# Three edits to the first layer of a fused three-layer kernel: gate projection placed before the recurrence, group norm regrouped, input squares summed by matmul

## The chip, the cores and the metric

The kernel runs on one core of a Trainium2 chip. The metric is device time in microseconds. Three executions took 2455.23, 2460.22 and 2460.65 us (median 2460.22). Five engines work side by side, each through its own queue in order, and meet through semaphores: TensorE (PE), VectorE (DVE), ScalarE (ACT), GpSimd (POOL) and SyncE (SP), which here only issues transfers.

## The reference

A sequence of 512 tokens of width 1024 goes through an RWKV-7 layer, an attention layer with forget gates and a hybrid layer, each with an MLP of width 4096. All is float32. Only the RWKV layer is changed. Cut to what matters:

```python
h = rmsnorm(x, g);  xx = shift(h) - h;  x_m = h + xx * mu[m]     # m: r w k v a g
r, k, v = x_r @ Wr, x_k @ Wk, x_v @ Wv
w = -softplus(-(w0 + tanh(x_w @ w1) @ w2)) - 0.5;  decay = exp(-exp(w))
a = sigmoid(a0 + (x_a @ a1) @ a2)
g = sigmoid(x_g @ g1) @ g2                    # rank 160, the output gate
kk = normalised(k * k_k);  k = k * (1 + (a - 1) * k_a);  b = kk * a
y  = scan(S -> S*w - (S@kk) b + v k, read with r)
y  = (y - mean) * rsqrt(var + eps) * lnx_w + lnx_b              # per head of 64
y  = (y + sum(r*k*r_k) * v) * g
x  = x + y @ w_o
```

## The kernel before

Activations are held turned: 8 tiles of 128 channels by 512 tokens. Every float32 product is made from three fast ones (`three`, lines 591 to 595): operands are split into a high and a low part, and high times high, high times low and low times high are added in PSUM. A projection of width 1024 is 8 weight blocks of 128x1024, and each block is one output tile of 24 matmuls (8 for k, times three), or, for k and r, one input tile against all 8 outputs.

Weights come as one stream of blocks. SP loads them into four slots `raw`; POOL splits each into one of two slots `whi`/`wlo` (lines 432 and 439), and may write a slot only when TensorE has finished the block two before it (semaphore `blk`). So the order of `PHASES` is the order of the weights on SP, POOL and TensorE.

The RWKV layer runs in stages, and each engine's order is written out by hand:

- **Input and low-rank projections.** ACT squares x into two buffers in turn (L1325) and makes the high part (L1326). DVE adds the squares into `ssq` (L1745) and makes the low part (L1776). TensorE makes the five blocks `lora` (w1 and a1 twice, g1 twice, the rest of g1), sums `ssq` over partitions (L599), then makes `lora_up` (L647 to 649), 16 tiles that ACT reads through a sigmoid (L1364). The first matmul waits for all constants (`const_in`).
- **k, r, v.** ACT and DVE build the mixed inputs (L1338, L1804, L1344, L1811); TensorE follows block by block. Between the value tiles stand head sums of squares and of the bonus (L605) and the spreading of the key norms over channels (`kk_spread`, L689). DVE then runs a chain over eight tiles (L1874 to L1886) that builds the keys, rates and queries and, for tiles 4 to 7, the bonus products (L1857).
- **Recurrence.** TensorE turns keys, rates and values to token order (L681), then runs four turns of chunked products with small copies by ACT and DVE.
- **Group norm and gate.** Means (L976), centring (L2019), squares (L1509), head sums (L605), square root (L1469), reciprocal (L1968). Then for each tile: spread the factor (L618), six matmuls of the gate's second projection, and on DVE scale, add bonus, multiply with the gate, low part (L2024, L2028, L2035, L2039); ACT applies the affine part and makes the high part.
- **Output projection** `rwkv_o`, 8 tiles through `linear`, with the residual added by DVE (L1955), and then the MLP.

## Time and profile before

| | |
|---|---|
| three executions, median | 2460.22 us |
| profiled execution, whole | 2465.94 us |
| its span in the trace | 2464.1 us |
| TensorE busy | 2354.1 us, 96% |
| mean granted TensorE clock | 0.975 of full speed |
| VectorE, GpSimd, ScalarE busy | 1189.3, 1289.0, 573.7 us |

The stages of the RWKV layer read off the timeline: low-rank projections to 62 us, k and r to 165, v and the key chain to 241, transposes to 259, recurrence to 458, group norm and gate to 512, output projection to 559. A time in brackets at a row's end is the idle time of the engine before that instruction, with what released it. PEclk is a share of 2.4 GHz.

### The profile page before, as it was taken

The numbers are of one execution on the slowest core, as the hardware profiler recorded it, in microseconds if no ns is written. First come the engines' busy times: TensorE is split into PE (matmuls) and PEld (weight loads), VectorE is DVE, ScalarE is ACT, GpSimd is POOL, SyncE is SP. The second block draws the span as 40 slices with busy tenths as digits, with TensorE's granted clock in tenths as the row PEclk, the third lists the DMA queues.
The fourth block names the chain that finished last, engine by engine and source line by source line (L and its number), as shares of the span: only waits on it lengthen the run. The fifth ranks groups of instructions, "written<-read, shape, count | busy, mean of one in ns | idle before, by whom it ended". The sixth has DMA issues, their size and how long they took to land.

```text
span 2464.1 us, 41824 instructions
## 1 busy us (share of the span) xinstructions
PE 2354.1 (96%) x16908; PEld 1886.9 (77%) x16908; DVE 1189.3 (48%) x1483; ACT 573.7 (23%) x1168; POOL 1289.0 (52%) x839
## 2 busy tenths in 40 slices
PE   6988999899999999989999999999999999999999
PEld 4765888578888877766788888787877777888887
DVE  8858433475343352667543334518045656633333
ACT  4541333221010122144311111101015441201100
POOL 4652001056666655555566666566544545666665
PEclk9998999879999999999999999999998998999999
DMA  3220000122223222201222322223321111222222
GB/s 143 83 72 25 3 3 3 69 68 95 94 94 102 94 91 76 89 20 35 69 94 95 101 94 94 94 94 112 111 85 44 44 35 66 96 96 94 99 96 85
DMA packets 50448, 188.37 MB, mean 76 GB/s; under 512 B 5617, under 2 KB 5745, under 8 KB 49809
## 3 DMA queue, kind: packets, MB, share of 16 engines
q1 hardware_dynamic: 49824, 183.40, 22.2%
q10 hardware_dynamic: 496, 3.12, 0.4%
q8 instruction: 99, 1.62, 0.3%
q14 instruction: 29, 0.23, 0.0%
HBM read 184.33 MB, written 2.10 MB: 76 GB/s over the span
## 4 chain that ended last, share of the span: by engine, by line
PE 85%; DVE 10%; issue 2%; ACT 2%; POOL 0%; DMA 0%; ACTq 0%; DVEq 0%; SPq 0%; POOLq 0%
PE ps L593 23%; PE ps L595 22%; PE ps L594 22%; PE ps L1099 2%; PE ps L1084 2%; PE ps L768 2%; PE ps L605 2%; DVE HL L1948 1%; PE ps L1065 1%; DVE ssq L1745 1%; PE ps L778 1%; PE ps L1066 1%; PE ps L776 1%; PE ps L761 1%; PE ps L754 1%
## 5 line engine op out<-in xcount | busy, mean ns | idle before, releaser
L439 POOL TENSOR_TENSOR wlo<-raw,whi 128x1024 fp32r<-128x1024 f32 (+1 forms) x355 | 828.3, 2333 | 26.4
L432 POOL TENSOR_SCALAR whi<-raw 128x1024 fp32r<-128x1024 f32 x336 | 362.5, 1079 | 816.9 <-PE ps L595 792.3
L593 PE MATMUL ps<-HH,whi 128*128 128x512 f32 x1312 | 529.7, 404 | 8.4 <-DVE HL L1948 8.4
L595 PE MATMUL ps<-HH,wlo 128*128 128x512 f32 x1312 | 514.3, 392 | 0.0
L594 PE MATMUL ps<-HL,whi 128*128 128x512 f32 x1312 | 513.9, 392 | 0.0
L593 PEld LDWEIGHTS ps<-HH,whi 128*128 128x128 f32 x1312 | 248.1, 189 | 69.8 <-DVE HL L1948 14.1
L593 PE MATMUL ps<-hidH,whi 128*128 128x512 f32 x768 | 298.8, 389 | 0.0
L594 PE MATMUL ps<-hidL,whi 128*128 128x512 f32 x768 | 298.8, 389 | 0.0
L595 PE MATMUL ps<-hidH,wlo 128*128 128x512 f32 x768 | 298.8, 389 | 0.0
L595 PEld LDWEIGHTS ps<-HH,wlo 128*128 128x128 f32 x1312 | 248.2, 189 | 52.9
L594 PEld LDWEIGHTS ps<-HL,whi 128*128 128x128 f32 x1312 | 248.6, 189 | 52.3 <-issue 4.3
L1995 DVE TENSOR_TENSOR X<-X,ps 128x512 f32<-128x512 f32 x192 | 123.3, 683 | 306.7 <-PE ps L595 306.7
L1481 ACT ACTIVATE sqrT<-relT 128x512 f32<-128x512 f32 x96 | 60.8, 634 | 792.0 <-DVE relT L1984 792.0
L1987 DVE TENSOR_TENSOR hidL<-sqrT,hidH 128x512 fp32r<-128x512 f32 x96 | 183.9, 1935 | 88.8 <-ACT hidH L1485 88.8
L1984 DVE SCALAR_TENSOR_TENSOR relT<-ps,rstd 128x512 f32<-128x512 f32 x96 | 66.4, 692 | 234.1 <-PE ps L595 234.0
L594 PEld LDWEIGHTS ps<-hidL,whi 128*128 128x128 f32 x768 | 144.2, 188 | 30.0
L595 PEld LDWEIGHTS ps<-hidH,wlo 128*128 128x128 f32 x768 | 144.2, 188 | 29.9
L593 PEld LDWEIGHTS ps<-hidH,whi 128*128 128x128 f32 x768 | 144.2, 188 | 29.9
L465 POOL TENSOR_TENSOR mRB<-mRB,cst 128x512 f32<-128x512 f32 x8 | 10.1, 1279 | 176.2 <-ACT mRB L1435 176.2
L494 POOL TENSOR_SCALAR prs<-prs,cls,GT 128x32 f32<-128x32 f32 (+4 forms) x48 | 32.9, 686 | 78.0 <-DVE cls L2122 66.0
L593 PE MATMUL ps<-mixH,whi 128*128 128x512 f32 x128 | 52.8, 412 | 11.8 <-DVE mixL L1811 8.9
L1310 ACT ACTIVATE HH<-X,vec 128x512 fp32r<-128x512 f32 x40 | 28.8, 721 | 144.0 <-DVE X L1955 71.2
(438 smaller groups left out, 3598.6 us busy)
## 6 DMA issues: line engine op xcount, KB each, us to landing
raw<-stream SPq DMA_DIRECT2D x336, 512.0 KB, 3.3
X<-xT SPq DMA_DIRECT2D x2, 1024.0 KB, 6.6
X<-xT SPq DMA_DIRECT2D x1, 2048.0 KB, 7.7
CW<-cmpw ACTq DMA_DIRECT2D x1, 2048.0 KB, 10.2
out<-X SPq DMA_DIRECT2D x4, 512.0 KB, 2.6
cst<-consts SPq DMA_DIRECT2D x1, 511.5 KB, 9.3
c2f<-consts ACTq DMA_DIRECT2D x1, 466.0 KB, 3.2
c2s<-consts ACTq DMA_DIRECT2D x1, 466.0 KB, 5.4
```

Of the source, the lines that this page charges most:

```text
L432: pool.tensor_scalar(whi[:, s, :, :], raw[:, j, :].rearrange("p (k m) -> p k m", k=DT), 1.0, 0.0, ALU.mult, ALU.add)\
L439: return pool.tensor_tensor(wlo[:, s, a:z, :], raw[:, j, a * P:z * P].rearrange("p (k m) -> p k m", k=z - a), whi[:, s, a:z, :].bitcast(F3 ...
L593: pe.matmul(acc, whi[:, s, k, :], hi, start=start, stop=False)
L594: pe.matmul(acc, whi[:, s, k, :], lo, start=False, stop=False)
L595: return pe.matmul(acc, wlo[:, s, k, :], hi, start=False, stop=stop)
L605: pe.matmul(ps[0:112, bank, :], gather_heads(i), tmp[i % 2][:, :], start=i == 0, stop=i == n - 1).then_inc(S(f"{tag}_sum"), 1)
L768: mm = pe.matmul(square(hp, 1 - c, hp, p), mN[half(c), hp, p, :], mT[half(c), hp, p, :], start=True, stop=True)
L1084: mm = pe.transpose(ps[0:w, 4 + hp, j * P:(j + 1) * P], B["P"][:, 2 * (u % 2) + hp, j * P:j * P + w], ident)
L1481: act.activation(sqrT[:, j % 2, :], relT[:, j % 2, :], ACT.Square).then_inc(S("full"), 1)
L1984: dve.scalar_tensor_tensor(relT[:, j % 2, :], ps[:, j, :], 0.0, rstd[:, :], ALU.max, ALU.mult).then_inc(S("rel"), 1)
L1987: dve.tensor_tensor(hidL[buf][:, j - 1, :], sqrT[:, (j - 1) % 2, :], hidH[buf][:, j - 1, :].bitcast(F32), ALU.subtract).then_inc(S("hid"), 1)
L1995: ins = dve.tensor_tensor(X[:, e, :], X[:, e, :], ps[:, 4 + 2 * (j % 2) + o, :], ALU.add)
```

## The change

1. **Input.** The squares are summed by eight float32 matmuls against a column of ones (`x_square`, the first four ahead of block 0, the others between its k-steps); DVE's eight additions and the wait for the constants are gone. The low-rank blocks come in two groups: three, then `lora_up`'s weights in buffers of their own (`upH`, `upL`), then two; eight tiles of `lora_up` follow the fourth block made and eight the fifth.
2. **Gate.** The sigmoid's high and low parts are made among the mixes, and the 48 matmuls of `gate_up` stand behind the last value tile and ahead of the transposes. ACT copies the result to `G`, which lies over the four `raw` slots, so the output projection's weights are loaded after the recurrence, each slot as its two tiles of `G` are read (`gn_a`). The head sums and spreads between the value tiles stand one or two tiles elsewhere (`BETWEEN`).
3. **Group norm.** DVE computes `BON = (BON + lnx_b) * G` within the recurrence, two tiles a turn. After it, `YA = centred * lnx_w * G`, then `YA * factor + BON`; ACT's affine step is gone. Means and head sums alternate. The first two tiles of `rwkv_o` are made side by side, one k-step as each low part of y is ready, with the spread of a later tile behind it.

```diff
-    ("lora", 5), ("lora_up", 1), ("k", DT), ("r", DT), ("v", DT), ("gate_up", 2),
+    ("lora_a", 3), ("lora_up", 1), ("lora_b", 2), ("k", DT), ("r", DT), ("v", DT), ("gate_up", 2),
...
+    upH = at("upH", [P, DT, P], zone(5, 2048), F32R)
+    upL = at("upL", [P, DT, P], zone(5, 6144), F32R)
...
+    G = at("G", full, zone(10))
+    YA = at("YA", full, zone(7))
...
+        SCALED = [0, 1, 2, 4, 5]
+        SLOT = {0: 0, 1: 1, 2: 0, 4: 1, 5: 0}
+        FREED = {2: 1, 4: 2, 5: 3, 6: 5, 7: 5}
...
             sp.wait_ge(S("rec_done"), 1)
-            sp.dma_start(X[:, :, :], xT).then_inc(S("x_again"), 16)
-            with sp.Fori(pre, NBLK // RAW) as i:
+            for j in range(RAW):
+                sp.wait_ge(*count("gn_a", 2 * j + 2))
+                sp.dma_start(raw[:, j, :], stream[pre * RAW + j]).then_inc(S(f"raw_in{j}"), 16)
+                if j == 1:
+                    sp.dma_start(X[:, :, :], xT).then_inc(S("x_again"), 16)
...
-            splits(2 * RAW, START["gate_up"])
+            splits(2 * RAW, START["rwkv_o"])
...
+            def x_square(i):
+                pe.wait_ge(S("norm_sq"), i + 1)
+                pe.matmul(ps[:, 4, :], unit[:, 0:1].to_broadcast([P, P]), tmp[i % 2][:, :], start=i == 0, stop=i == DT - 1)\
+                    .then_inc(S("norm_sum"), 1)
+            def lora_up(first, end):
+                if first == 0:
+                    pe.wait_ge(S("split_ready"), START["lora_up"] + 1)
+                    pe.wait_ge(S("lo_split"), 1)
+                    pe.wait_ge(S("norm_root"), 1)
+                for t in range(first, end):
+                    e, m = divmod(t, 2)
+                    r = slice(m * LORA, m * LORA + LORA)
+                    if t >= len(UP_BANKS):
+                        pe.wait_ge(S("lora_read"), t - len(UP_BANKS) + 1)
+                    acc = ps[:, UP_BANKS[t % len(UP_BANKS)], :]
+                    pe.matmul(acc, upH[r, e, :], loH[r, :], start=True, stop=False)
+                    pe.matmul(acc, upH[r, e, :], loL[r, :], start=False, stop=False)
+                    mm = pe.matmul(acc, upL[r, e, :], loH[r, :], start=False, stop=True)
+                    mm.then_inc(S("blk") if t == 15 else S("lora_up"), 1)
+            pe.wait_ge(S("consts_set"), 1)
+            for i in range(4):
+                x_square(i)
+            for n, b in enumerate(SCALED):
                 pe.wait_ge(S("split_ready"), b + 1)
                 for k in range(DT):
-                    if b == 0:
+                    if n == 0:
                         pe.wait_ge(S("x_lo"), k + 1)
-                    mm = three(ps[:, LORA_BANKS[b], :], (b % SPL, k), XH[:, k, :], XL[:, k, :], k == 0, k == DT - 1)
+                    mm = three(ps[:, LORA_BANKS[n], :], (SLOT[b], k), XH[:, k, :], XL[:, k, :], k == 0, k == DT - 1)
+                    if n == 0 and k < 4:
+                        x_square(4 + k)
                 mm.then_inc(S("blk"), 1)
-                if b == 0:
-                    norm_mean(0)
...
+                if n >= 3:
+                    lora_up(8 * (n - 3), 8 * (n - 2))
...
-            BETWEEN = [("kk", 0, 4), ("kk", 4, 8), ("bo", 0, 2), ("bo", 2, 4), ("bo", 4, 6), ("bo", 6, 8)]
+            BETWEEN = [("kk", 0, 4), ("kk", 4, 8), None, ("bo", 0, 2), ("bo", 2, 4), ("bo", 4, 6), ("bo", 6, 8), None]
...
+            g0 = START["gate_up"]
+            pe.wait_ge(S("split_ready"), g0 + 2)
+            pe.wait_ge(S("sg_split"), 1)
+            for e in range(DT):
+                if e < 2:
+                    pe.wait_ge(S("rkv_read"), 16 + 5 + e)
+                else:
+                    pe.wait_ge(S("g_copied"), e - 1)
+                mm = three(ps[:, e % 2, :], (g0 % SPL, e), sgH[:, 0, :], sgL[:, 0, :], True, False)
+                if e == 7:
+                    mm.then_inc(S("blk"), 1)
+                mm = three(ps[:, e % 2, :], ((g0 + 1) % SPL, e), sgH[:, 1, :], sgL[:, 1, :], False, True)
+                mm.then_inc(S("gate_up") if e < 7 else S("blk"), 1)
...
+            pe.wait_ge(S("y_done"), NCH)
+            for i in range(DT + 3):
+                if i < DT:
+                    if i >= 4:
+                        pe.wait_ge(S("gn_c"), i - 3)
+                    pe.matmul(ps[:, i % 4, :], const("bones"), Rr[:, i, :], start=True, stop=True).then_inc(S("gn_mean"), 1)
+                if i >= 3:
+                    head_sum("gn", i - 3, DT)
+            def y_tile(e, bank, k):
+                mm = three(ps[:, bank, :], ((START["rwkv_o"] + e) % SPL, k), YH[:, k, :], YL[:, k, :], k == 0, k == DT - 1)
+                if k == DT - 1:
                     mm.then_inc(S("blk"), 1)
-                mm = three(ps[:, 6 + e % 2, :], ((g0 + 1) % SPL, e), sgH[:, 1, :], sgL[:, 1, :], False, True)
-                mm.then_inc(S("gate_up") if e < 7 else S("blk"), 1)
+            for i in range(3):
+                spread("gn", i, [2, 3], gnR)
+            ready(START["rwkv_o"] + 1)
+            for k in range(DT):
+                pe.wait_ge(S("y_lo"), k + 1)
+                for e in range(2):
+                    y_tile(e, e, k)
+                if k + 3 < DT:
+                    spread("gn", k + 3, [2, 3], gnR)
             pe.wait_ge(*count("gn_used", DT))
-            linear("rwkv_o", YH, YL, ("y_lo", 0), ("x_up", 0), [])
+            for e in range(2, DT):
+                ready(START["rwkv_o"] + e)
+                if e >= 4:
...
-            act.wait_ge(S("h_ready"), DT)
             for t in range(16):
                 e, m = divmod(t, 2)
                 if t < 15:
                     act.wait_ge(S("lora_up"), t + 1)
                 else:
-                    act.wait_ge(S("blk"), START["lora_up"] + 1)
-                mark(act.activation((DEC, AG)[m][:, e, :], ps[:, UP_BANKS[t % len(UP_BANKS)], :], ACT.Sigmoid,
+                    act.wait_ge(S("blk"), START["k"])
+                if m:
+                    act.wait_ge(S("h_ready"), e + 1)
+                mark(act.activation((Rr, AG)[m][:, e, :], ps[:, UP_BANKS[t % len(UP_BANKS)], :], ACT.Sigmoid,
                                bias=vcol(("w0", "a0")[m], e)), "lora_read")
-                if t == 11 or t == 13:
-                    mix_hi((t - 11) // 2)
+                if t == 7:
+                    mix_hi(0)
+                    mix_hi(1)
...
+                    link(act.activation(sgF[:, :, :], sgF[:, :, :], ACT.Sigmoid), "sg_ready")
+                    mark(act.activation(sgH[:, :, :], sgF[:, :, :], ACT.Copy), "sg_hi")
...
+            act.wait_ge(S("split_ready"), START["rwkv_o"])
+            for e in range(DT):
+                if e < 7:
+                    act.wait_ge(S("gate_up"), e + 1)
+                else:
+                    act.wait_ge(S("blk"), START["gate_up"] + 2)
+                mark(act.activation(G[:, e, :], ps[:, e % 2, :], ACT.Copy), "g_copied")
...
                 x_lo(i)
                 if i == 3:
                     mixed_weights(1)
             mixed_weights(2)
+            mixed_weights(3)
             norm_recip(0)
-            mixed_weights(3)
+            mixed_weights(4)
+            for i in range(2):
+                normed(i)
             for b in range(2):
                 dve.wait_ge(S("blk"), b + 1)
                 link(dve.tensor_tensor(loF[:, :] if b == 0 else loS[:, 0, :], ps[:, b, :], rstd[:, :], ALU.mult))
             mark(dve.tensor_tensor(loF[:, 1:T], loF[:, 1:T], loS[:, 0, 0:T - 1], ALU.add), "lo_f")
-            mixed_weights(4)
+            for i in range(2, 4):
+                normed(i)
             dve.wait_ge(S("lo_h"), 1)
             mark(dve.tensor_tensor(loL[:, :], loF[:, :], loH[:, :].bitcast(F32), ALU.subtract), "lo_split")
-            for i in range(DT):
-                mark(dve.scalar_tensor_tensor(H[:, i, :], X[:, i, :], vcol("norm_g", i), rstd[:, :], ALU.mult, ALU.mult), "h_ready")
+            for i in range(4, DT):
+                normed(i)
             dve.wait_ge(S("h_ready"), 8)
...
+                if n == 8:
+                    dve.wait_ge(S("sg_hi"), 1)
+                    mark(dve.tensor_tensor(sgL[:, :, :], sgF[:, :, :], sgH[:, :, :].bitcast(F32), ALU.subtract), "sg_split")
...
+                if n == 0:
+                    dve.wait_ge(S("g_copied"), DT)
+                for i in (2 * n, 2 * n + 1):
+                    link(dve.scalar_tensor_tensor(BON[:, i, :], BON[:, i, :], vcol("lnx_b", i), G[:, i, :], ALU.add, ALU.mult))
...
-            dve.wait_ge(S("sg_hi"), 1)
-            mark(dve.tensor_tensor(sgL[:, :, :], sgF[:, :, :], sgH[:, :, :].bitcast(F32), ALU.subtract), "sg_split")
+            def gated(i):
+                mark(dve.scalar_tensor_tensor(YA[:, i, :], Rr[:, i, :], vcol("lnx_w", i), G[:, i, :], ALU.mult, ALU.mult), "gn_a")
             for i in range(DT):
                 dve.wait_ge(S("gn_mean"), i + 1)
-                mark(dve.scalar_tensor_tensor(Rr[:, i, :], ps[:, i % 2, :], -1.0 / HD, Rr[:, i, :], ALU.mult, ALU.add), "gn_c")
+                mark(dve.scalar_tensor_tensor(Rr[:, i, :], ps[:, i % 4, :], -1.0 / HD, Rr[:, i, :], ALU.mult, ALU.add), "gn_c")
+            dve.wait_ge(S("gn_c"), DT)
+            for i in range(4):
+                gated(i)
             head_recip("gn", gnR)
             for n in range(DT + 2):
                 if n < DT:
+                    dve.wait_ge(*count("gn_a", n + 1))
                     dve.wait_ge(*count("gn_spread", n + 1))
-                    mark(dve.tensor_tensor(Rr[:, n, :], Rr[:, n, :], ps[:, 2 + n % 2, :], ALU.mult), "gn_used")
+                    mark(dve.tensor_tensor(YA[:, n, :], YA[:, n, :], ps[:, 2 + n % 2, :], ALU.mult), "gn_used")
+                if n + 4 < DT:
+                    gated(n + 4)
                 i = n - 1
                 if 0 <= i < DT:
-                    dve.wait_ge(S("gn_aff"), i + 1)
-                    link(dve.tensor_tensor(Rr[:, i, :], Rr[:, i, :], BON[:, i, :], ALU.add))
-                    if i < 7:
-                        dve.wait_ge(S("gate_up"), i + 1)
-                    else:
-                        dve.wait_ge(S("blk"), START["gate_up"] + 2)
+                    dve.wait_ge(*count("gn_used", i + 1))
                     if i >= 2:
-                        dve.wait_ge(S("y_hi"), i - 1)
-                    mark(dve.tensor_tensor(tmp[i % 2][:, :], Rr[:, i, :], ps[:, 6 + i % 2, :], ALU.mult), "y_gated")
+                        dve.wait_ge(S("y_lo"), i - 1)
+                    mark(dve.tensor_tensor(tmp[i % 2][:, :], YA[:, i, :], BON[:, i, :], ALU.add), "y_gated")
                 i = n - 2
                 if 0 <= i:
                     dve.wait_ge(S("y_hi"), i + 1)
```

TensorE's queue, behind the value tiles. `cst,Kk` are the transposes of the keys, `mixVH`/`mixVL` the values' input. Before:

```order
L593 MATMUL ps<-mixVH,whi 128x512
L594 MATMUL ps<-mixVL,whi 128x512
L595 MATMUL ps<-mixVH,wlo 128x512
L681 MATMUL ps<-cst,Kk 128x128 x32
L681 MATMUL ps<-cst,AG 128x128 x32
L718 MATMUL ps<-boR,pselR 128x512
L681 MATMUL ps<-cst,Vv 128x128 x4
```

The transposes follow the last value tile directly.

Of the change, in TensorE's queue where the gate begins:

```order
L612 MATMUL ps<-mixVH,whi 128x512
L613 MATMUL ps<-mixVL,whi 128x512
L614 MATMUL ps<-mixVH,wlo 128x512
L612 MATMUL ps<-sgH,whi 128x512
L613 MATMUL ps<-sgL,whi 128x512
L614 MATMUL ps<-sgH,wlo 128x512
```

And where it ends:

```order
L612 MATMUL ps<-sgH,whi 128x512
L613 MATMUL ps<-sgL,whi 128x512
L614 MATMUL ps<-sgH,wlo 128x512
L712 MATMUL ps<-cst,Kk 128x128 x32
L712 MATMUL ps<-cst,AG 128x128 x32
L762 MATMUL ps<-boR,pselR 128x512
L712 MATMUL ps<-cst,Vv 128x128 x4
```

The 48 rows with `sgH` and `sgL` stand between the last value tile and the transposes.

TensorE's queue after the head sums of the group norm; `gnR,pselR` is the spread of a factor, `YH`/`YL` the parts of y. Before:

```order
L618 MATMUL ps<-gnR,pselR 128x512
L593 MATMUL ps<-sgH,whi 128x512
L594 MATMUL ps<-sgL,whi 128x512
L595 MATMUL ps<-sgH,wlo 128x512
L593 MATMUL ps<-sgH,whi 128x512
L594 MATMUL ps<-sgL,whi 128x512
L595 MATMUL ps<-sgH,wlo 128x512
L618 MATMUL ps<-gnR,pselR 128x512
L593 MATMUL ps<-sgH,whi 128x512
```

A spread and six gate matmuls alternate. TensorE's queue of the change there:

```order
L637 MATMUL ps<-gnR,pselR 128x512 x3
L612 MATMUL ps<-YH,whi 128x512
L613 MATMUL ps<-YL,whi 128x512
L614 MATMUL ps<-YH,wlo 128x512
L612 MATMUL ps<-YH,whi 128x512
L613 MATMUL ps<-YL,whi 128x512
L614 MATMUL ps<-YH,wlo 128x512
L637 MATMUL ps<-gnR,pselR 128x512
L612 MATMUL ps<-YH,whi 128x512
L613 MATMUL ps<-YL,whi 128x512
```

The six matmuls between two spreads no longer use the gate's input, which was ready, but y, tile by tile.

VectorE's queue in the same place. Before, tiles 0 to 3:

```order
L2024 TENSOR_TENSOR KR<-KR,ps 128x512 x2
L2028 TENSOR_TENSOR KR<-KR,BON 128x512
L2035 TENSOR_TENSOR tmpA<-KR,ps 128x512
L2024 TENSOR_TENSOR KR<-KR,ps 128x512
L2028 TENSOR_TENSOR KR<-KR,BON 128x512
L2035 TENSOR_TENSOR tmpB<-KR,ps 128x512
L2039 TENSOR_TENSOR YL<-tmpA,YH 128x512
L2024 TENSOR_TENSOR KR<-KR,ps 128x512
L2028 TENSOR_TENSOR KR<-KR,BON 128x512
L2035 TENSOR_TENSOR tmpA<-KR,ps 128x512
```

VectorE's queue of the change, from the spread of tile 1 to that of tile 4:

```order
L2102 SCALAR_TENSOR_TENSOR YA<-KR,vec,G 128x512
L2123 TENSOR_TENSOR tmpA<-YA,BON 128x512
L2115 TENSOR_TENSOR YA<-YA,ps 128x512
L2102 SCALAR_TENSOR_TENSOR YA<-KR,vec,G 128x512
L2123 TENSOR_TENSOR tmpB<-YA,BON 128x512
L2127 TENSOR_TENSOR YL<-tmpA,YH 128x512
L2115 TENSOR_TENSOR YA<-YA,ps 128x512
L2102 SCALAR_TENSOR_TENSOR YA<-KR,vec,G 128x512
L2123 TENSOR_TENSOR tmpA<-YA,BON 128x512
L2127 TENSOR_TENSOR YL<-tmpB,YH 128x512
L2115 TENSOR_TENSOR YA<-YA,ps 128x512
```

The low part `YL` of a tile is the last instruction before the scaling of the tile two further on, which reads the next spread.

## Rows read from the trace of the kernel before

**Rows 1.** The page: busy time per engine, and the chain's shares.
```profile
PE 2354.1 (96%) x16908; PEld 1886.9 (77%) x16908; DVE 1189.3 (48%) x1483; ACT 573.7 (23%) x1168; POOL 1289.0 (52%) x839
...
PE 85%; DVE 10%; issue 2%; ACT 2%; POOL 0%; DMA 0%; ACTq 0%; DVEq 0%; SPq 0%; POOLq 0%
```

**Rows 2.** Windows of the first layer: length, engines' busy time (count), TensorE clock, DMA.
```profile
62.17:70.20 8.03, 8.03 (x25) 6.43 (x26) 2.99 (x5) 1.16 (x2) 1.19 (x1) 0.70 0.19 65
70.20:164.80 94.60, 85.71 (x360) 67.72 (x359) 79.09 (x59) 54.52 (x83) 59.55 (x30) 0.98 0.23 79
164.80:240.90 76.10, 65.46 (x233) 43.80 (x231) 52.94 (x72) 12.60 (x21) 25.14 (x14) 0.93 0.12 41
...
458.10:474.60 16.50, 15.24 (x32) 4.88 (x32) 6.57 (x9) 6.08 (x10) 0.00 (x0) 1.00 0.65 254
474.60:480.70 6.10, 0.01 (x1) 0.04 (x1) 5.15 (x4) 0.67 (x1) 0.00 (x0) 0.66 0.00 0
480.70:509.40 28.70, 28.67 (x56) 16.80 (x56) 18.37 (x28) 10.92 (x15) 1.03 (x1) 0.50 0.00 0
509.40:512.25 2.85, 0.00 (x0) 0.03 (x1) 2.85 (x2) 0.00 (x0) 2.77 (x3) 0.50 0.00 0
520.40:525.90 5.50, 5.50 (x26) 4.57 (x25) 0.69 (x1) 1.25 (x2) 3.46 (x2) 1.00 0.11 22
...
512.25:558.60 46.35, 46.35 (x194) 38.12 (x195) 32.63 (x24) 9.35 (x15) 30.00 (x16) 0.94 0.29 93
```

**Rows 3.** Timeline, TensorE: start, length (us), line, operation, [idle before, releaser].
```profile
15.92 0.80 PE L593 MATMUL ps<-XH,whi 128*128 128x512 f32 x1 [15.92 <-DMA pselF<-consts]
...
26.65 1.02 PE L599 MATMUL ps<-ssq,cst 128*128 128x512 f32 x2
...
62.17 0.80 PE L593 MATMUL ps<-mixH,whi 128*128 128x512 f32 x1 [2.96 <-ACT AG L1364]
```

**Rows 4.** Timeline, ScalarE, table load ahead of the sixteen sigmoids.
```profile
50.43 1.28 ACT L1364 ACT_TABLE_LOAD   x1 [8.85 <-PE ps L649]
```

**Rows 5.** Timeline, VectorE, the sum of squares.
```profile
10.63 2.83 DVE L1745 TENSOR_TENSOR ssq<-ssq,tmpB 128x512 f32<-128x512 f32 x1
...
14.04 0.68 DVE L1745 TENSOR_TENSOR ssq<-ssq,tmpA 128x512 f32<-128x512 f32 x1
```

**Rows 6.** Timeline, GpSimd, the first split's low half.
```profile
10.26 2.65 POOL L439 TENSOR_TENSOR wlo<-raw,whi 128x1024 fp32r<-128x1024 f32 x1
```

**Rows 7.** Timeline, TensorE, between the value tiles and the transposes.
```profile
209.80 2.05 PE L605 MATMUL ps<-tmpB,cst 128*112 128x512 f32 x2 [5.08 <-DVE tmpB L1857]
...
240.95 4.26 PE L681 MATMUL ps<-cst,Kk 128*128 128x128 f32 x22 [4.70 <-DVE boR L1861]
```

**Rows 8.** Timeline, VectorE, two starts in the key chain.
```profile
198.01 0.69 DVE L1874 TENSOR_TENSOR KR<-KR,ps 128x512 f32<-128x512 f32 x1 [3.33 <-PE ps L689]
...
212.61 0.69 DVE L1874 TENSOR_TENSOR KR<-KR,ps 128x512 f32<-128x512 f32 x1 [1.06 <-PE ps L689]
```

**Rows 9.** Timeline, VectorE, one turn of the recurrence.
```profile
289.43 1.28 DVE L1933 TENSOR_TENSOR mRK<-ps,cst 128x512 f32<-128x512 f32 x2
294.19 0.69 DVE L1938 COPY mN<-ps 64x512 f32<-64x512 f32 x1 [3.48 <-PE ps L845]
```

**Rows 10.** Timeline, VectorE, the group norm.
```profile
475.30 3.35 DVE L1968 RECIPROCAL rstd<-rstd 112x512 f32<-112x512 f32 x1 [7.42 <-ACT rstd L1469]
478.69 0.43 DVE L1971 CAST gnR<-rstd 112x512 fp32r<-112x512 f32 x1
479.15 1.40 DVE L1861 TENSOR_TENSOR gnR<-rstd,gnR 16x512 fp32r<-16x512 f32 x2
...
485.07 0.69 DVE L2024 TENSOR_TENSOR KR<-KR,ps 128x512 f32<-128x512 f32 x1 [2.89 <-PE ps L618]
```

**Rows 11.** Timeline, GpSimd, the first split of the output projection's weights.
```profile
508.37 1.04 POOL L432 TENSOR_SCALAR whi<-raw 128x1024 fp32r<-128x1024 f32 x1 [90.25 <-PE ps L595]
509.50 2.65 POOL L439 TENSOR_TENSOR wlo<-raw,whi 128x1024 fp32r<-128x1024 f32 x1
```

126 lines of the change are left out of this document (57 added, 69 removed).

## Prediction

> **What bounds the kernel now.** I read the page first: TensorE is busy 96% of the span and 85% of the chain of waits runs over it [rows 1]. So time comes from TensorE's gaps, its matmuls at the lower clock and work taken off it. The change takes little off: the 48 gate matmuls are moved, not dropped. Its touched stages lie in the first 559 us, so next I cut these into windows [rows 2]. They show:
>
> - To 62.17 us TensorE starts late: its first matmul waits 15.92 us for a table that only a later stage needs, and the k projection waits 2.96 us for the last sigmoid, then runs at half clock [rows 3].
> - From 70.2 to 164.8 us TensorE works 85.7 of 94.6 us and VectorE 79.1: the two pace each other.
> - From 164.8 to 240.9 us TensorE works 65.5 of 76.1 us. It waits 5.08 us in the middle and 4.70 us at the end, both for VectorE's key chain [rows 7].
> - The group norm and gate take 16.5 + 6.1 + 28.7 + 2.85 us. The granted clock is 0.50, 1.2 GHz, during all 28.7 us of the gate, though TensorE is busy for 28.67 of them. It first rises in the output projection.
>
> Costs used throughout, from these windows: a tile of 24 matmuls takes 5.5 us at 2.4 GHz, so 0.23 us a matmul; at 1.2 GHz six matmuls and a spread take 28.7/8 = 3.6 us, so 0.43 us a matmul. The sum is made against the profiled execution, 2465.94 us (span 2464.1 us and 1.8 us around it), which lies 5.7 us above the median of 2460.22. I take 5.7 off at the end.
>
> **Part 1, the input.** VectorE's eight additions go: 0.68 us each, but 2.83 us where GpSimd's low half of a split (2.65 us) runs under it [rows 5, 6]. In their place come eight float32 matmuls of about 0.9 us, twice that at 1.2 GHz (1.02 us for the one in [rows 3], 2.05 us for another at the lower clock in [rows 7]). TensorE may start with the first square, and four of these at 1.2 GHz, 7.4 us, are over before block 0 can run freely. That block is paced by the low parts of x. VectorE is free of the first split at 13.46 us [rows 5], makes two low parts at 0.68 and scales the second block's weights in twice 0.6, to 16.0; their split of 1.04 and 2.65 us [rows 11] and its handovers end near 20.1. The last two low parts queue behind it, to 21.5, and block 0 ends at 22.3. Before, it ended at 26.65 and the sum's own matmul took it to 27.1: 4.8 us gained. Four blocks of 5.5 us stand behind it in both. The sixteen low-rank tiles need a table load of 1.28 us [rows 4] and sixteen reads; before they cost 13.2 us (from 27.1 + 4 x 5.47 = 49.0 to 62.17), of which TensorE waits 2.96 us at the end. In two groups I count 4.7 us for the first (load, then waits for three banks) and 6.4 us for the second, 11.1 together; the other reads lie under the fifth block. With 0.6 us for the fourth block's split, k starts at 56.0 instead of 62.17. Its first block took 8.03 us at a mean clock of 0.70; with a gap of only 0.7 us ahead of it I count 5.5, 2.5 us less. Sum 8.6 us.
>
> Everything up to 164.8 us follows that block, through the mixes. One instruction comes into VectorE's chain, the gate input's low part over 1024 columns: twice 0.68, 1.3 us; its high part lies in ScalarE's idle time. **Input: -7.3 us**, bounds -4 (VectorE is late again elsewhere) and -9.
>
> **Part 2, the gate ahead of the transposes.** The last value tile ended at 240.95 - 4.70 = 236.25 us. Two things change behind it. First, the head sums come later and the bonus products reuse their buffers: bonus 4 now waits for the third head sum, which stands behind the fifth value tile. VectorE waits there some 2 us, and TensorE then waits for VectorE's second and fourth tiles at the spreads, 4.5 and 5 us instead of 5.08 us once. The chain is also relieved: it no longer stands still until 212.61 [rows 8]. On balance I put the last value tile's end at 238.8. Second, the gate needs both its weight blocks split, and the second may be split only when that tile is done: 1.04 + 2.65 us [rows 11] and 0.1, so it starts at 242.6. VectorE's key chain ends meanwhile and is no longer late. 48 matmuls at 0.23 are 11.0 us, and a gap of 3.8 us costs me half clock for the first eleven, 2.2 us: 255.8. ScalarE copies a tile while the next one's six matmuls run, 1.4 us. The transposes began at 240.95, so +14.9 us; they then no longer run at half clock at their start (22 passes took 4.26 us), worth about 1.9. **Gate: +13 us.** Low bound +7: TensorE's waits at the two spreads do not arise and the gap keeps the clock. High bound +22: all 48 at 0.43 us, 20.6 us.
>
> **Part 3, within the recurrence.** Two instructions of 0.68 us a turn. VectorE is idle 3.48 us behind its last mask [rows 9], and TensorE waits for the mask, not for what follows. **0 us**; without that cover 1.4 us a turn, 5.6 us.
>
> **Part 4, group norm and first two output tiles.** Means and head sums alternate: 15.24 us of work in 16.5 us, so 1.2 us earlier to the square root. Reciprocal, cast and low rows follow (3.35, 0.43, 1.40 us [rows 10]). But the output projection's weights are loaded only now, behind `gn_a`, and the first split's low half runs from about 476.4 to 479 us, under the cast. In rows 5 and 6 such an instruction ends only when GpSimd's does. That takes the 1.2 us back, and the second split holds the scaling of tile 4 by another 1.2: first spread at 480.7 as before, first low part of y at 488.7.
>
> The Trainium skill (GPSIMD Engine Reference, Specifications) says that GpSimd shares its SBUF interfaces with VectorE and contends with instructions that have two SBUF inputs. The stretched addition, two SBUF inputs, agrees. By this rule the new products with `G` and `BON` are open to it, where the product with the gate read PSUM.
>
> From there the order makes a ring. VectorE's queue puts the low part of a tile ahead of the next scaling but one, which waits for a spread, and TensorE puts that spread behind the six matmuls that wait for this low part. Nothing in it overlaps. A turn costs TensorE 3.6 us at 1.2 GHz and VectorE three instructions and their handovers, 2.05 us; the first has one more, 2.65. Five turns: 6.25 + 4 x 5.65 = 28.9 us, to 517.6 (before, a turn was the 3.6 us alone). The last three k-steps are 18 matmuls, begun at 1.2 GHz, 6.8 us: 524.4. The third tile needs a split that may begin only when the first is complete, 0.7 us earlier: 1.04 + 2.65 us, so 527.4. Before, it began at 512.25 + 8.15 + 5.50 = 525.9. That is +1.5, and I add 1 for a clock that may fall in this gap. **Group norm: +2.5 us**, bounds -9 (rival A) and +5. The six tiles behind it and all later layers stay.
>
> **Sum.** -7.3 + 13 + 0 + 2.5 = +8.2 us: 2474.1 for the profiled execution, 2468 beside the median.
>
> **The rivals.**
>
> A. The clock comes back inside the ring. At 2.4 GHz TensorE's share of a turn is about 2.1 us, five turns take 21.4 us, the rest 4.4, and the third tile starts near 517: -9 instead of +1.5, and nothing for a cold restart. The sum is then -3 or so, 2457. For it: the clock rose within the first tile of the output projection, after a pause. Against it: TensorE streamed 28.7 us without one rise, and in the ring it stands 2 us or more in each turn.
>
> The Trainium skill (TensorE: Matmul & The Clock Gate, Part 1) holds that sustained activity releases the throttle. By it this rival would hold more readily; the gate's window at 0.50 while busy speaks against taking it so simply.
>
> B. The value tiles lose no time: the key chain gains what the bonus waits cost. Gate +7, sum +2, 2462. For it: the stop until 212.61 goes. Against: a value tile is 5.5 us, and each new wait moves a whole one.
>
> C. A and B together, the case on the other side: -7.3 + 7 - 9 = -9, 2451. It is decided at the ring: only if its turns fall under 5 us does the change win.
>
> D. The gate stays at 1.2 GHz in its new place as in its old: +9 more, 2477. For it: the old window, where half of the matmuls have weights that are zero in 96 of 128 rows. Against: there a spread of 48 rows breaks each group of six, and here none does; the output projection, without spreads, recovered.
>
> **How the numbers follow.** The forecast 0.46 (its own range 2463 to 2474), A 0.15, B 0.15, C 0.12, D 0.12. A measurement of this kernel tells about 0.3% from no change, 7.4 us: below 2452.8 is faster, above 2467.6 slower. Faster: most of C and a little of A, 0.15. Same: the rest of A and C, most of B and the lower fifth of the forecast, 0.37. Slower: the rest, 0.48. Range 2453 to 2480.
>
> **What would show it.** Right: k starts near 56 us at full clock; the last value tile ends within 4 us of 231 (238.8 less 7.3), a gap of some 3.8 us under GpSimd, then 48 matmuls in 11 to 14 us; the recurrence is as long as before, 199 us; turns of 5.5 to 6 us in the group norm at clock 0.50, TensorE waiting for `YL` in each. Wrong: turns near 4 us at clock 1.00 (A), TensorE without waits at the third and fifth spread of the key norms (B), 20 us for the gate (D), or k starting after 60 us, which would leave nothing of part 1.

## The result and the profile after

| | before | after |
|---|---|---|
| median of the executions | 2460.06 us (5, 2453.27 to 2460.65) | 2472.01 us (5, 2469.28 to 2472.47) |
| profiled execution | 2465.94 us | 2472.37 us |
| its span | 2464.1 us | 2470.6 us |

The change makes the kernel slower, by about half a percent: ratio 1.0057, 95% interval 1.0042 to 1.0071 (ratios and intervals are taken over the single executions and can differ a little from the quotient of the medians, which is 1.0049 here, 12.0 us). The forecast was 2468.0 us in a range of 2453 to 2480, with slower as the likeliest side. One execution of the first edit alone (2639.8 us, clock 0.839) and one of the gate buffer kernel (6428.6 us) lay far above all others and are in no ratio below.

From the page of the changed kernel, the lines that answer to [rows 1]: busy time per engine, and the chain's shares.

```profile
PE 2352.3 (95%) x16922; PEld 1886.8 (76%) x16922; DVE 1196.8 (48%) x1484; ACT 571.0 (23%) x1168; POOL 1289.2 (52%) x839
...
PE 86%; DVE 9%; issue 2%; ACT 1%; POOL 1%; DMA 0%; ACTq 0%; DVEq 0%; SPq 0%; POOLq 0%
```

TensorE is as busy as before. Next its windows, in the columns of [rows 2]: the k projection's first block, the value tiles, the gap ahead of the gate, the gate, the recurrence, the wait ahead of the first spread, the wait ahead of the first y matmul, and the eight steps of the first two output tiles. The columns are: start and end of the window, its length, the busy time and number of instructions of PE, PEld, DVE, ACT and POOL, the mean clock granted to TensorE, and the transfers' share and rate.

```profile
56.45:63.59 7.14, 7.14 (x25) 5.79 (x26) 3.50 (x4) 1.11 (x2) 2.19 (x1) 0.77 0.35 120
...
159.94:235.40 75.46, 66.86 (x233) 45.57 (x231) 50.98 (x62) 11.87 (x20) 28.87 (x16) 0.91 0.12 41
235.40:239.67 4.27, 0.02 (x2) 0.00 (x1) 4.24 (x5) 0.60 (x1) 3.88 (x2) 1.00 0.00 0
239.67:252.34 12.67, 12.67 (x49) 10.22 (x50) 3.84 (x7) 4.18 (x7) 0.00 (x0) 0.87 0.00 0
...
259.71:465.12 205.41, 198.24 (x6761) 172.76 (x6760) 82.83 (x125) 71.46 (x127) 10.06 (x8) 1.00 0.01 3
...
479.30:489.36 10.06, 0.00 (x1) 0.00 (x1) 9.15 (x4) 0.69 (x1) 7.22 (x4) 0.69 0.80 305
489.36:496.08 6.72, 2.01 (x3) 0.81 (x4) 5.68 (x9) 1.26 (x2) 0.00 (x0) 0.50 0.22 78
496.08:529.80 33.72, 22.79 (x53) 14.20 (x53) 12.42 (x20) 3.78 (x6) 0.21 (x1) 0.59 0.13 47
```

What [rows 2] had as 28.7 us of gate at clock 0.50 is now 12.67 us at 0.87 in another place; in its stead stand 33.72 us of y steps with TensorE busy for 22.79 of them at clock 0.59. The starts in the two profiled executions:

| start of | before | after | this stage adds | predicted |
|---|---|---|---|---|
| k projection | 62.17 | 56.45 | -5.7 | -6.2 |
| value tiles | 164.83 | 159.94 | +0.8 | -1.2 |
| transposes | 240.95 | 252.34 | +16.3 | +14.9 |
| bonus spreads | 249.75 | 259.71 | -1.4 | -1.9 |
| means (recurrence over) | 458.12 | 465.12 | -3.0 | 0 |
| first spread | 480.69 | 489.36 | +1.7 | 0 |
| third output tile | 525.9 | 533.21 | -1.4 | +1.5 |
| MLP | 558.36 | 567.59 | +1.9 | +1 |
| end of the span | 2464.1 | 2470.6 | -2.7 | 0 |

To the MLP the sum is +9.2 us where +8.2 was predicted. The -2.7 us behind it lie in stages that the change does not touch; "Before, again" below shows where. The timeline of TensorE in the changed kernel (start, length, line, operation, idle before and releaser) shows its waits, answering to [rows 3], [rows 7] and [rows 10]:

```profile
56.45 0.77 PE L612 MATMUL ps<-mixH,whi 128*128 128x512 f32 x1 [1.96 <-ACT AG L1424]
203.71 0.79 PE L720 MATMUL ps<-kkR,pselR 48*128 48x512 f32 x1 [4.33 <-DVE KR L1956]
219.15 0.79 PE L720 MATMUL ps<-kkR,pselR 48*128 48x512 f32 x1 [4.27 <-DVE KR L1956]
239.67 0.50 PE L612 MATMUL ps<-sgH,whi 128*128 128x512 f32 x1 [4.25 <-POOL wlo L454]
489.36 1.22 PE L637 MATMUL ps<-gnR,pselR 48*128 48x512 f32 x2 [10.06 <-DVE gnR L1943]
496.08 0.77 PE L612 MATMUL ps<-YH,whi 128*128 128x512 f32 x1 [4.29 <-DVE YL L2127]
502.41 0.80 PE L612 MATMUL ps<-YH,whi 128*128 128x512 f32 x1 [2.71 <-DVE YL L2127]
508.12 0.80 PE L612 MATMUL ps<-YH,whi 128*128 128x512 f32 x1 [2.05 <-DVE YL L2127]
513.82 0.80 PE L612 MATMUL ps<-YH,whi 128*128 128x512 f32 x1 [2.05 <-DVE YL L2127]
533.21 0.47 PE L612 MATMUL ps<-YH,whi 128*128 128x512 f32 x1 [3.17 <-POOL wlo L454]
```

The waits at two spreads of the key norms (L720, 4.33 and 4.27 us), the 4.25 us for GpSimd ahead of the gate, and turns of 6.33, 5.71, 5.70 us with a wait for `YL` in each are the steps the prediction named. VectorE in the same stage, first its factor chain, then one turn (compare [rows 10]):

```profile
480.06 3.35 DVE L2054 RECIPROCAL rstd<-rstd 112x512 f32<-112x512 f32 x1 [0.86 <-ACT rstd L1538]
483.44 1.67 DVE L2057 CAST gnR<-rstd 112x512 fp32r<-112x512 f32 x1
485.15 4.15 DVE L1943 TENSOR_TENSOR gnR<-rstd,gnR 16x512 fp32r<-16x512 f32 x2
...
506.17 0.69 DVE L2115 TENSOR_TENSOR YA<-YA,ps 128x512 f32<-128x512 f32 x1 [3.81 <-PE ps L637]
506.78 0.68 DVE L2123 TENSOR_TENSOR tmpB<-YA,BON 128x512 f32<-128x512 f32 x1
507.38 0.68 DVE L2127 TENSOR_TENSOR YL<-tmpA,YH 128x512 fp32r<-128x512 f32 x1
```

GpSimd's timeline, the low halves beside the chain (compare [rows 11]):

```profile
482.49 2.34 POOL L454 TENSOR_TENSOR wlo<-raw,whi 128x1024 fp32r<-128x1024 f32 x1
...
486.10 2.65 POOL L454 TENSOR_TENSOR wlo<-raw,whi 128x1024 fp32r<-128x1024 f32 x1
```

The cast took 0.43 us before and the two low rows 1.40; now, with both low halves of the splits beside them, 1.67 and 4.15. The reciprocal kept its 3.35 us although the first low half began under its end.

### The profile page after: what moved, and what is told of

Read it like the earlier page. It is cut to its first block, busy times and chain, and to the rows that moved or that the text cites. A ratio compares the mean times of both kernels' runs of the same rounds, so it can differ in the third digit from the quotient of the medians.

```text
span 2470.6 us, 41859 instructions
## 1 busy us (share of the span) xinstructions
PE 2352.3 (95%) x16922; PEld 1886.8 (76%) x16922; DVE 1196.8 (48%) x1484; ACT 571.0 (23%) x1168; POOL 1289.2 (52%) x839
## 3 DMA queue, kind: packets, MB, share of 16 engines
q1 hardware_dynamic: 49824, 183.40, 22.2%
## 4 chain that ended last, share of the span: by engine, by line
PE 86%; DVE 9%; issue 2%; ACT 1%; POOL 1%; DMA 0%; ACTq 0%; DVEq 0%; SPq 0%; POOLq 0%
PE ps L612 23%; PE ps L613 23%; PE ps L614 23%; PE ps L1140 2%; PE ps L1155 2%; PE ps L812 2%; PE ps L624 1%; DVE HL L2034 1%; PE ps L1121 1%; PE ps L822 1%; PE ps L1122 1%; PE ps L820 1%; PE ps L805 1%; DVE ssq L1809 1%; PE ps L798 1%
## 5 line engine op out<-in xcount | busy, mean ns | idle before, releaser
L513 POOL TENSOR_SCALAR prs<-prs,cls,GT 128x32 f32<-128x32 f32 (+4 forms) x48 | 32.9, 684 | 78.2 <-DVE cls L2210 66.2
```

## Experiments

All are compared with executions of the kernel before on their own chip (the column "before" is its median there). These medians run from 2456.9 to 2459.8 us, so a difference of 2 or 3 us between two kernels that ran on different chips is not shown by their medians alone. The changed kernel again, products early, sums as before, and ring open kept busy shared one chip; first edit alone, ring open, gate buffer and splits late shared another; all four mended, mended kept busy, and before again a third. Theory after the comparison: three sizeable costs, each from one order or buffer (the ring of turns; the split that waits for the last value tile; head sums a tile later), one from GpSimd beside VectorE's factor chain, and a first edit that gains. Rivals stand in the expectations.

| kernel | median us (executions) | before | ratio, 95% interval |
|---|---|---|---|
| changed, again | 2470.89 (6) | 2456.92 | 1.0046 [1.0029, 1.0064] |
| first edit alone | 2453.69 (12) | 2459.17 | 0.9980 [0.9968, 0.9993] |
| ring open | 2455.49 (12) | 2459.17 | 0.9997 [0.9981, 1.0012] |
| gate buffer | 2466.20 (12) | 2459.17 | 1.0035 [1.0023, 1.0046] |
| splits late | 2470.99 (6) | 2459.17 | 1.0051 [1.0034, 1.0068] |
| products early | 2468.50 (8) | 2456.92 | 1.0045 [1.0029, 1.0061] |
| sums as before | 2467.61 (9) | 2456.92 | 1.0037 [1.0023, 1.0050] |
| ring open, kept busy | 2455.07 (12) | 2456.92 | 0.9990 [0.9979, 1.0000] |
| all four mended | 2448.67 (6) | 2459.18 | 0.9954 [0.9938, 0.9971] |
| mended, kept busy | 2437.39 (4) | 2459.18 | 0.9913 [0.9898, 0.9927] |
| before, again | 2459.68 (8) | 2459.18 | 1.0004 [0.9992, 1.0016] |
| first edit, kept busy | 2446.12 (6) | 2459.78 | 0.9944 [0.9930, 0.9958] |

**First edit alone.** The changed kernel with its second and third edit taken back: gate, `BETWEEN`, `G`, the product into `BON` and the group norm as in the kernel before.

```diff
-            splits(2 * RAW, START["rwkv_o"])
+            splits(2 * RAW, START["gate_up"])
...
```

> The kernel before with the first edit alone (squares summed by TensorE, low-rank blocks in two groups); gate and group norm as before. Theory (the parts add up, and part 1 is worth what the value tiles' start shows, 159.9 us after against 164.8 before, with 1.3 us more since the gate input's low part is not in VectorE's mix chain here): value tiles begin near 158.6 to 159.9, everything behind is shifted by that, and the time is 5 to 6 us under the kernel before, about 2455. k starts near 56.4 us at clock 0.50 for some 3 us. Rival 1 (the first edit's gain is given back in the key chain, whose waits are set by GpSimd and not by when the mixes end): value tiles begin early but the transposes begin as before, 0 to -2 us. Rival 2 (the prediction's 7.3 us is there once the low part is gone): -7 us, 2453.

It gains 5.5 us. Value tiles began at 158.16 us, the transposes at 234.27 instead of 240.95: nothing is given back in the key chain, rival 1 falls. In the variants below that keep the gate input's low part among the mixes the value tiles begin at 158.0 to 158.5 too, in seven of nine profiled executions (the other two, at 159.6 and 159.7, are taken up under "Changed kernel, again"), so that low part costs nothing; 1.3 us had been charged for it.

**Ring open.** Four banks for the spreads, four of them ahead of the first y matmul.

```diff
+        GN_BANKS = [2, 3, 6, 7]
-            for i in range(3):
-                spread("gn", i, [2, 3], gnR)
+            for i in range(4):
+                spread("gn", i, GN_BANKS, gnR)
...
-                if k + 3 < DT:
-                    spread("gn", k + 3, [2, 3], gnR)
+                if k + 4 < DT:
+                    spread("gn", k + 4, GN_BANKS, gnR)
```

> The changed kernel with four PSUM banks for the group norm's spreads instead of two: four spreads ahead of the first y matmul, the spread of tile k+4 behind k-step k. Nothing else differs. Theory (a turn is long because VectorE's scaling of tile k+3 waits for a spread that stands behind the matmuls that wait for its own earlier low part): TensorE's six k-step turns fall from 5.6 to 6.3 us to the 3.4 us of their matmuls at 1.2 GHz, the eight k-steps end near 520 instead of 529.8, and the time falls by some 10 us to 2462; if the clock also comes back, VectorE's 2.05 us a turn is the limit and it falls by 15 to 17, to 2456. Rival (the low parts themselves come late, by the chain add, high part, low part across two engines, 2.7 us for a tile): the waits for YL stay at about 2 us a turn and the gain is under 3 us, 2470.

Its window of the eight y steps, in the same columns as above:

```profile
491.64:514.10 22.46, 22.43 (x52) 14.54 (x52) 12.48 (x20) 3.78 (x6) 0.50 (x1) 0.57 0.20 70
```

The steps take 22.46 us instead of 33.72, TensorE stands in none of them, and a step with its spread is 3.58 us, at clock 0.57. The ring is shown, and it is the largest cost of the change: 11.3 us in the steps. The time is 16.5 us under the changed kernel's first median and 15.4 under its second, but not all of that is the ring's. Of the 16.4 us between the two profiled executions 4.9 lie ahead of the first spread, where nothing was edited: 2.7 of them came by the last value tile's end, where fewer stretches at half clock fell, and 1.8 are VectorE's factor chain, whose low rows met the second split otherwise:

```profile
482.27 2.13 DVE L1944 TENSOR_TENSOR gnR<-rstd,gnR 16x512 fp32r<-16x512 f32 x2
```

They took 4.15 us in the changed kernel, and 4.16 in ring open, kept busy. In the trace the ring is worth 11 us, not 15.

**Gate buffer.** The gate's second block is split into bytes that the sigmoid's input and the key factors have left.

```diff
+    gbH = at("gbH", [P, DT, P], zone(8), F32R)
+    gbL = at("gbL", [P, DT, P], zone(8, 4096), F32R)
...
+                if own:
+                    pool.wait_ge(S("sg_split"), 1)
+                    pool.wait_ge(S("k_scaled"), DT)
```

> The changed kernel with a buffer of its own for the gate's second weight block, so that its split no longer waits for the last value tile. Theory (the 4.25 us gap ahead of the gate is only that split, and half clock over the gate's first matmuls follows from the gap): gap under 0.7 us, 48 matmuls in 11 us instead of 12.7, transposes begin near 247 instead of 252.3, VectorE's key chain, which ended at 243.6, is still in time; time falls by 4 to 6 us, to 2467. Rival (VectorE's key chain becomes the bound, since the split now runs against it earlier): the transposes wait for VectorE and the gain is under 2 us, 2471.

TensorE's first gate matmul:

```profile
233.04 0.50 PE L625 MATMUL ps<-sgH,whi 128*128 128x512 f32 x1 [0.33 <-POOL gbL L472]
```

The wait is 0.33 us instead of 4.25; the 48 matmuls take 11.0 us (233.04 to 244.07) instead of 12.67. Measured 4.7 to 5.8 us less in the medians, and the transposes begin 5.5 us earlier than in ring open (244.07 against 249.58), whose value tiles began at the same time: the theory holds, VectorE's chain stayed in time.

**Splits late.** GpSimd waits for the factor rows.

```diff
+            pool.wait_ge(*count("gn_root", 2))
             splits(START["rwkv_o"], START["kv_v"] + 4)
```

> The changed kernel, in which GpSimd begins the output projection's first splits only when VectorE has made the group norm's factor rows. Theory (VectorE's cast, 1.67 us, and two low rows, 4.15 us, are stretched by the splits beside them; before they took 0.43 and 1.40): they take 0.43 and 1.40 again, the first spread starts near 485.4 instead of 489.4, the first y matmul near 493.2 where the second split ends instead of 496.1, and the time falls by 2 to 3 us to 2469.5. Rival (the cast and the rows are slow for another reason, such as their own semaphores or the four products before them): both stay as long, the splits begin 4 us later and the time rises by 1 to 2 us, 2473.5.

VectorE's factor rows and first products, from its timeline:

```profile
482.43 0.43 DVE L2058 CAST gnR<-rstd 112x512 fp32r<-112x512 f32 x1
482.89 1.40 DVE L1944 TENSOR_TENSOR gnR<-rstd,gnR 16x512 fp32r<-16x512 f32 x2
...
485.85 2.90 DVE L2103 SCALAR_TENSOR_TENSOR YA<-KR,vec,G 128x512 f32<-128x512 f32 x1
...
490.11 2.82 DVE L2124 TENSOR_TENSOR tmpA<-YA,BON 128x512 f32<-128x512 f32 x1
```

And GpSimd's low halves:

```profile
485.86 2.34 POOL L454 TENSOR_TENSOR wlo<-raw,whi 128x1024 fp32r<-128x1024 f32 x1
...
489.74 2.65 POOL L454 TENSOR_TENSOR wlo<-raw,whi 128x1024 fp32r<-128x1024 f32 x1
```

The first half of the theory is shown: 0.43 and 1.40 us without GpSimd beside them, first spread 20.2 us behind the means instead of 24.2. The second half is wrong: the splits now stretch a product (0.74 us without them) to 2.90 and an addition (0.68) to 2.82, and the first y matmul still comes 31.4 us behind the first mean (31.0 in the changed kernel). The time is the changed kernel's. A stretch that is moved is not a stretch removed.

**Products early.** VectorE's first four products with `G` go into its 1.03 us pauses between centrings, so the slots come free and both splits end earlier.

```diff
                 mark(dve.scalar_tensor_tensor(Rr[:, i, :], ps[:, i % 4, :], -1.0 / HD, Rr[:, i, :], ALU.mult, ALU.add), "gn_c")
-            dve.wait_ge(S("gn_c"), DT)
-            for i in range(4):
-                gated(i)
+                if i >= 4:
+                    dve.wait_ge(S("gn_c"), i - 3)
+                    gated(i - 4)
```

> The changed kernel with VectorE's first four products with G placed in its idle time between the centrings instead of behind them, so that the weights' slots come free and their splits end earlier. Theory (GpSimd's low halves stretch VectorE instructions with two SBUF inputs to 2.1 to 2.9 us wherever both meet, and not the reciprocal, which has one): the first low half lies before, the second under the reciprocal, so cast and low rows take 0.43 and 1.40 us again, and nothing is stretched later, as it was in the run with late splits; first spread 4 us earlier against the means, first y matmul 4 us earlier, 2467 where the changed kernel gives 2471. Rival 1 (the stretch moves to the products and centrings that now meet the splits): gain under 1.5 us. Rival 2 (the products delay the centrings and with them the square root): 0 or slower.

VectorE's factor chain in this kernel:

```profile
480.30 3.35 DVE L2054 RECIPROCAL rstd<-rstd 112x512 f32<-112x512 f32 x1 [2.98 <-ACT rstd L1538]
483.68 1.16 DVE L2057 CAST gnR<-rstd 112x512 fp32r<-112x512 f32 x1
484.88 1.40 DVE L1943 TENSOR_TENSOR gnR<-rstd,gnR 16x512 fp32r<-16x512 f32 x2
```

GpSimd's second low half lay at 482.22 to 484.56, for the larger part under the reciprocal, which keeps 3.35 us; only the cast is still caught (1.16). First spread 21.0 us behind the first mean instead of 24.3 in the changed kernel, again. The median falls by 2.4 us against the changed kernel on the same chip; the intervals overlap, so that the trace, not the time, carries this.

**Sums as before.** The order of the kernel before between the value tiles.

```diff
-            BETWEEN = [("kk", 0, 4), ("kk", 4, 8), None, ("bo", 0, 2), ("bo", 2, 4), ("bo", 4, 6), ("bo", 6, 8), None]
+            BETWEEN = [("kk", 0, 4), ("kk", 4, 8), ("bo", 0, 2), ("bo", 2, 4), ("bo", 4, 6), ("bo", 6, 8), None, None]
```

> The changed kernel with the head sums between the value tiles in the order of the kernel before (bonus sums from the third tile on). Theory (the eight value tiles and their sums take 74.2 us instead of 71.0 because the fourth and sixth tile's successors wait 4.3 us twice for VectorE, whose bonus products wait for sums that stand a tile later): one wait goes, the last value tile ends 3 us earlier, gate and all behind it follow, 2468. Rival (the waits come from GpSimd's splits stretching VectorE's key chain, and sit elsewhere in either order): the value stage stays within 1 us, 2471.

TensorE's waits over the whole value stage:

```profile
203.57 2.05 PE L624 MATMUL ps<-tmpB,cst 128*112 128x512 f32 x2 [5.14 <-DVE tmpB L1939]
223.86 0.49 PE L720 MATMUL ps<-kkR,pselR 48*128 48x512 f32 x1 [0.91 <-DVE KR L1956]
```

5.14 and 0.91 us instead of 4.33 and 4.27, and no other. From the first value tile to the last one's end the stage takes 71.5 us instead of 75.5; 3.3 us less in the median (again inside the overlap of intervals). The seven profiled executions with the changed order took 74.5 to 75.5 us there, the seven with the old order 71.2 to 71.5. That this order alone costs the value stage 3 to 4 us is shown.

**Ring open, kept busy.** Superfluous matmuls while TensorE waits.

```diff
+            for i in range(9):
+                pe.matmul(ps[:, 4, :], const("bones"), Rr[:, 0, :], start=True, stop=True)
             for i in range(4):
                 spread("gn", i, GN_BANKS, gnR)
+            for i in range(5):
+                pe.matmul(ps[:, 4, :], const("bones"), Rr[:, 0, :], start=True, stop=True)
```

> The kernel with four banks for the spreads (2455.5 us), to which 14 superfluous float32 matmuls of 0.86 us are added into an unused bank: nine ahead of the first spread and five ahead of the first y matmul, where TensorE waits 8.2 and 5.1 us. They are extra work whose result nobody reads. Theory (TensorE runs the first five y steps at 1.2 GHz because it stood still before them): the granted clock stays at or near 1.00, a step costs 2.1 us (VectorE's three instructions then pace it) instead of 3.58, the y steps end 6 to 8 us earlier, 2449. Rival 1 (the clock falls all the same, or falls in the short waits of the steps): steps of 3.6 us, and the time is unchanged or up to 2 us longer where the extra matmuls overrun their gap, 2456 to 2458. Rival 2 (full clock but VectorE stretched): 2452.

TensorE's timeline: the nine matmuls (as eighteen passes), two steps, and the third output tile:

```profile
477.21 7.89 PE L1033 MATMUL ps<-KR,cst 128*128 128x512 f32 x18
487.42 1.20 PE L638 MATMUL ps<-gnR,pselR 48*128 48x512 f32 x4 [2.32 <-DVE gnR L1948]
...
498.23 0.50 PE L613 MATMUL ps<-YH,whi 128*128 128x512 f32 x1
500.35 0.50 PE L613 MATMUL ps<-YH,whi 128*128 128x512 f32 x1
...
512.07 0.77 PE L613 MATMUL ps<-YH,whi 128*128 128x512 f32 x1 [3.17 <-POOL wlo L454]
```

The clock did stay up: steps of 2.12 us instead of 3.58. But VectorE's factor chain, beside the splits, took as long as in the changed kernel, 1.8 us more than in the execution of ring open; the recurrence took 1.2 us more; and behind the last step TensorE again waited 3.17 us for a split and began the third tile at clock 0.53 over 5.9 us. Of 7.4 us gained in the steps 3.6 remained between the two profiled executions, and of the medians, from two chips, only 0.4 (each against its own before: kept busy 1.9 us under it, ring open 3.7). So the cause of the slow steps was right, and no gain in the time is shown; part of it was lost behind the place that was mended, and where the rest went the traces do not say.

**Changed kernel, again.**

> The changed kernel, nothing altered, beside the others on one chip. Theory (the two profiled executions that were compared are each untypical: the one of before holds two stretches of half clock, in the recurrence and in the last layer, that cost 3 us each; the one of the changed kernel began the k projection at half clock, where four variants of it began at full clock and reached the value tiles at 158.1 to 158.3 instead of 159.9): value tiles begin near 158.2, the transposes near 250.5 and the time is 2469 to 2471, 10 to 12 us above before. Rival (the half clock belongs to the changed kernel): value tiles at 159.9 again, 2472.

Value tiles at 159.69, transposes at 251.99, 2470.9 us: the rival, if either. The profiled execution, 2475.6 us, lies 4.7 us above its median; its y steps took 34.7 us. My reading that variants began the k projection at full clock was of their first three matmuls only; in all of them the first block took 7.0 to 7.2 us, with some 3 us at half clock. (Of the kernels below, the one with all four mended is an exception: 5.52 us at clock 1.00, behind the same wait of 1.96 us.) What differs between executions is where further stretches of half clock fall: with the first edit, the value tiles began at 159.6 to 159.9 in three executions and at 158.0 to 158.5 in the nine others. From 147.33 to 159.94 us the clock was 0.86 in the changed kernel's first execution, one of the three, and 1.00 in ring open's.

**Before, again.**

> The kernel before, nothing altered, for a second profiled execution of it. Theory (its first profiled execution, 2465.94 us against a median of 2457 to 2460, holds two stretches at half clock which belong to that execution alone: in the recurrence near 410 us, clock 0.94 over 30 us, and near 1850 us, 3 us each): at least one of the two stretches is gone and the recurrence from the first bonus spread to the first mean takes 205.4 us, as in the changed kernel, instead of 208.4. Rival (they belong to the kernel before, whose recurrence VectorE leaves otherwise): 208.4 again.

The recurrence took 206.2 us, so 2.2 of the 3.0 us that the first comparison seemed to give the change there belonged to one execution. The half clock near 1850 us was there again: between two of TensorE's waits that end near 1846 and 1875 us in the first execution of the kernel before, the fourteen profiled executions of this study took 28.4 us in six cases and 25.4 in eight, whatever the kernel. Both executions of the kernel before are among the six and both of the changed kernel among the eight; this is the -2.7 us behind the MLP in the table of starts, and why the two kernels fall so is open. And in the gate loop, TensorE's spreads, and the two windows that meet where the clock rises:

```profile
489.36 0.79 PE L618 MATMUL ps<-gnR,pselR 48*128 48x512 f32 x1
492.94 0.79 PE L618 MATMUL ps<-gnR,pselR 48*128 48x512 f32 x1
495.36 0.49 PE L618 MATMUL ps<-gnR,pselR 48*128 48x512 f32 x1
497.43 0.49 PE L618 MATMUL ps<-gnR,pselR 48*128 48x512 f32 x1
```

```profile
478.65:493.90 15.25, 15.25 (x30) 8.91 (x31) 7.95 (x13) 5.14 (x7) 0.00 (x0) 0.50 0.00 0
493.90:502.55 8.65, 7.76 (x27) 4.60 (x27) 8.54 (x14) 4.82 (x7) 0.41 (x1) 1.00 0.00 0
```

Turns of 3.58 us become 2.07 to 2.5 some 15 us after the first spread: here the clock does rise within the loop, which [rows 2] showed at 0.50 for all 28.7 us. From first spread to MLP this execution takes 73.0 us, the first took 77.7. The changed kernel's two took 78.2 and 80.1. Against this execution of before, the changed kernel, again, reaches the MLP 18.7 us later, not 9.2: how large the group norm's loss looks depends on which execution of before is taken.

**All four mended, and mended with TensorE kept busy.** The four edits above together; then eighteen superfluous matmuls, nine and five placed as in ring open, kept busy, and these four.

```diff
             pe.wait_ge(*count("gn_used", DT))
+            for i in range(4):
+                pe.matmul(ps[:, 4, :], const("bones"), cst[:, 0:T], start=True, stop=True)
             for e in range(2, DT):
```

> The changed kernel with all four mendings: four banks for the spreads, own buffer for the gate's second block, early products with G, head sums in the order of before. Theory (four separate costs at four places, each measured alone against 2470.9 us: -15.4, -4.7, -2.4 and -3.3): they add to 26, 2445, some 12 us under before and 9 under the first edit alone; turns near 3.6 us, gate right behind the last value tile, transposes near 241.5. Rival 1 (the key chain on VectorE, which before ended 4.7 us behind the last value tile, is now late for the transposes, since the gate starts 9 us earlier): they wait 1 to 3 us, 2447 to 2448. Rival 2 (the costs overlap): 2450 or more.

> The same with 18 superfluous float32 matmuls into an unused bank in TensorE's waits of the group norm: nine ahead of the first spread, five ahead of the first y matmul, four behind the last of the first two output tiles. Theory (clock 1.00 through the stage where TensorE does not stand still): y steps of 2.1 us instead of 3.6 for the first five, third output tile at full clock; 6 to 8 us less, 2438. Rival (the extra matmuls overrun their gaps, which the earlier factor chain has made 3 to 4 us shorter, and delay the first spread and first y step by what they overrun): the gain is 2 to 4 us, 2442.

The window of the y steps with all four mended:

```profile
483.16:505.30 22.14, 22.04 (x52) 14.30 (x52) 12.55 (x21) 3.78 (x6) 0.56 (x1) 0.58 0.21 71
```

And kept busy:

```profile
482.71:500.90 18.19, 17.36 (x61) 10.74 (x61) 15.32 (x22) 6.16 (x10) 3.52 (x3) 1.00 0.25 86
```

All four mended: 2448.7 us, 22.2 less than the changed kernel where the separate gains sum to 25.8 (that sum counts the 3 to 5 us that came with ring open and are not the ring's), 0.46% under before. Kept busy it is 2437.4, 11.3 us less again, more than was expected: clock 1.00 instead of 0.58 in the steps, and the output tiles behind them begin at full clock (clock 1.00 instead of 0.95 to the MLP). Between the profiled executions, 10.7 us apart, 8.9 lie between first spread and MLP. It is the fastest of all, 0.9% under before.

**First edit, kept busy.** Seven superfluous matmuls ahead of the old gate loop.

```diff
             head_sums("gn", DT)
+            for i in range(7):
+                pe.matmul(ps[:, 4, :], const("bones"), Rr[:, 0, :], start=True, stop=True)
```

> The kernel before with the first edit alone (2453.7 us, its gate loop at 1.2 GHz over all eight turns, 3.58 us each), to which seven superfluous float32 matmuls into an unused bank are added in TensorE's 6.15 us wait ahead of the first spread. Gate and group norm stand as before. Theory (the old gate loop was slow for the wait ahead of it and not for its 48-row spreads or its place): clock 1.00 through the loop, turns of 2.1 to 2.7 us, paced by VectorE's four instructions, 7 to 10 us less, 2445; the mended order with extra matmuls (2437.4) is then ahead by the rest, the moved gate's own worth. Rival (the loop's spreads keep the clock down, as the prediction supposed): turns stay near 3.6 us and the time is unchanged, 2454.

The window over the gate loop of the first edit alone:

```profile
470.21:500.00 29.79, 28.68 (x56) 16.80 (x56) 19.45 (x29) 10.92 (x15) 2.02 (x2) 0.50 0.00 1
```

Of this kernel:

```profile
472.00:496.00 24.00, 18.32 (x61) 11.44 (x62) 22.35 (x32) 11.58 (x16) 6.37 (x4) 0.95 0.04 13
```

And from its timeline two of its spreads:

```profile
471.53 0.47 PE L631 MATMUL ps<-gnR,pselR 48*128 48x512 f32 x1
473.51 0.49 PE L631 MATMUL ps<-gnR,pselR 48*128 48x512 f32 x1
```

Turns of 2.0 to 2.5 us instead of 3.58, from the first on, with the same spreads of 48 rows: the loop was slow for the wait ahead of it. 7.6 us less in the median. The mended kernel with TensorE kept busy is 8.7 us faster still. Not all of this is the worth of the second and third edit once their own costs are gone: of 9.4 us between the two profiled executions 5.2 are there at the MLP, and 3.0 are the stretch near 1850 us. Some of the 5.2 is clock as well, since here a wait of 3.83 us ahead of the output projection was left unfilled and the window from 493.72 to 500.00 us ran at 0.73. A kernel of the first edit with this wait filled too was not run.

## Why the prediction was right, and where it was not

The side and the forecast case came true. The time was met within 4 us; the change of it was 12.0 us between the medians where 7.8 was forecast, and part of the agreement is luck, as the steps show:

- **Part 1, -7.3 us.** k at 56.45 us against 56.0. "I count 5.5" for the first block failed: it took 7.14 us. The gap ahead of it is 1.96 us, not 0.7, since TensorE again ends ahead of ScalarE's last sigmoid; the wait became shorter, not small. The 1.3 us for the low part was charged for nothing (first edit alone). Both errors nearly cancel: -6.3 to -6.8 us at the value tiles in most variants, and -4.9 in the profiled execution, which had a further stretch of half clock ahead of them. TensorE's blocks, not the low parts of x, pace block 0: its first five k-steps are 1.55 us apart with a sum of squares between.
- **Part 2, +13 us: 14.9 measured.** Last value tile predicted within 4 us of 231.5, ended at 235.4; waits of 4.5 and 5 predicted, 4.33 and 4.27 came; gap 3.8 against 4.25; gate 13.2 against 12.67; transposes 1.9 against 1.4 less. What was undersized is what the later head sums cost beside the rest: 3 to 4 us of the value stage, where the balance had 2.55.
- **Part 3, 0.** The recurrence read 3.0 us shorter; 2.2 of that were gone with another execution of the kernel before. Nothing suggests a cost.
- **Part 4, +2.5: 2.2 measured**, mostly by luck. It was set against an execution of before whose gate loop stayed at half clock throughout; against the second one, whose clock came back, the changed kernel's first execution loses 5.3 us from first spread to MLP and not 0.6, so part 4 is near +7. Turns of 6.33, 5.71 and 5.70 us against 6.25 and 5.65 at clock 0.59: the ring was read from the order of two queues and is the best of the prediction. But the factor chain grew by 4.0 us, not 1.2: the contention was seen and put under too few instructions, since both low halves lie over cast and rows. The alternating sums gained 2.3 us, not 1.2, and the first low part came 6.7 us behind the first spread, not 8.0.
- **From the profile to the median.** The predicted profiled execution was 2474.1, and 2472.4 came. The median was put 5.7 us below, as in the kernel before, and lies only 0.4 below: this is the larger part of the miss of 4 us. The offset was no constant of the measurement. The second profiled execution of before lies 0.4 us below its median, 6.7 us under the first; half clock in the recurrence (2.2 us) and a gate loop that stayed slow throughout (4.7) account for that difference, while the stretch near 1850 us was in both. The changed kernel has no loop of this kind, but its second profiled execution lies 4.7 us above its median, so that its 0.4 is no constant either.
- **Rivals.** A, B and C did not come (clock 0.59 in the ring, both waits there), nor D: the gate ran at 0.87. The reason given against D, and for the half clock in the old loop, that spreads of 48 rows break the stream, is refuted by the last experiment. The Trainium skill's rule (TensorE: Matmul & The Clock Gate, Part 1) that sustained activity releases the throttle is borne out in part: in the old gate loop the clock came back after 15 us in one execution, and not in 28.7 us in another.
- **The rule on GpSimd** (the Trainium skill, GPSIMD Engine Reference, Specifications) agrees: the stretched products, additions and low rows have two SBUF inputs, and the reciprocal, with one, is not stretched. The cast has one as well and was stretched from 0.43 to 1.67 us. The prediction gave only half of the rule: the same section of the Trainium skill also names VectorE instructions in a 2-port perf mode. Whether the cast ran in such a mode no row of this case shows.

## What to carry to other kernels

Where two engines hand tiles to each other, write both queues side by side and look for an instruction that waits for one queued behind its own consumer: a second pair of buffers undid that here, worth 11 us in the trace. Read off, for each stretch at half clock, which wait stands ahead of it; filling that wait was worth more than moving the work (7.6 us on the first edit alone, where the second and third edit, mended, gave 5.0). And before subtracting a profile's offset from a median, look for the stretches at half clock that make it.

## What the runs showed of the hardware

- Superfluous matmuls in waits of 5 to 8 us kept the granted clock at 1.00 through the stage behind it (y steps 2.1 instead of 3.6 us, gate turns 2.0 to 2.5 instead of 3.58). Unfilled, the wait of 6.15 us ahead of the gate loop was followed by 1.2 GHz for 15 us in one execution and through the whole loop in two. One of 1.96 us ahead of the k projection was followed by some 3 us of it in eleven of twelve executions, and by none in the twelfth.
- The same loop of the same kernel ran at 0.50 for 28.7 us in one execution and came back after 15 us in another. The kernel before spreads over 14 us (2451.5 to 2465.5 in 29 executions). Twelve executions of ring open spread over 13.0 us, twelve with its waits filled over 5.5; that the clock makes this difference is likely but not shown.
- A low half of a split on GpSimd (2.3 to 2.7 us) added about 2.1 us to a VectorE instruction that began beside it: sum of squares 2.83 for 0.68, product 2.90 for 0.74, addition 2.82 for 0.68. Each of the three ended 0.54 to 0.55 us behind the end of the low half (13.46 behind 12.91, 488.75 behind 488.20, 492.93 behind 492.39). It did not touch the reciprocal (3.35 us in every profiled execution).
